# Eight sample sequences computed as a 17th chunk of the prompt's mixer stages

## The reference, cut to what matters

```python
# gated delta rule, for each chunk c of a sequence
m_low = jnp.where(strict, einsum('nbhik,nbhjk->nbhij', kb, k) * decay, 0.0)
sol = triangular_solve(m_low + eye(c), concatenate([v * beta, kb * exp(G)], -1))
v_new = uc - wc @ S                        # S: the state
o = (qc * exp(Gc)) @ S + ac @ v_new        # ac = mask(q k^T) * decay
S = S * exp(g_last) + (kc * exp(g_last - Gc))^T @ v_new
# mLSTM
num = w_inter * (qc @ cs) + s @ vc         # s = (q k^T) * exp(dc - mt)
den = w_inter * (qc @ ns) + sum(s)
cs, ns = a_end * cs + (kc * wk)^T @ vc, a_end * ns + (kc * wk)^T @ 1
```

## Time and profile before

| what | value |
|---|---|
| median of 3 executions | 2635.62 us (2635.26 to 2638.98) |
| the profiled execution, its own time | 2634.22 us |
| its span in the trace | 2632.6 us |
| mean granted TensorE clock | 0.847 of full speed |
| TensorE busy, weight loads busy | 2036.5 us (77%), 1684.9 us (64%) |
| VectorE, ScalarE, GpSimd busy | 1031.5, 488.8, 530.9 us |
| DMA | 117.75 MB, mean 45 GB/s |

### The profile page before, as it was taken

One profiled execution on the slowest core, in us unless ns is written; L12 is line 12 of the kernel. 1 busy time (PEld: TensorE's weight loads), 2 busy tenths in 40 slices (PEclk: granted clock), 3 DMA queues, 4 the chain that ended last, 5 costly groups with the idle time before them and its releaser, 6 DMA issues.

```text
span 2632.6 us, 28198 instructions
## 1 busy us (share of the span) xinstructions
PE 2036.5 (77%) x9888; PEld 1684.9 (64%) x9888; DVE 1031.5 (39%) x1987; ACT 488.8 (19%) x1073; POOL 530.9 (20%) x507
## 2 busy tenths in 40 slices
PE   5877786786534339599869885587899999999996
PEld 3544454454334338588846554464899999999995
DVE  4656665566458957323221401115311111111135
ACT  2211011111312123111120112102320310311311
POOL 0011110111134326110000000000433333433431
PEclk9988888888767669566679996678999999999998
DMA  3000000000042222111151000021111111111111
GB/s 109 32 20 28 18 28 18 18 22 20 10 89 59 39 33 56 62 37 54 36 209 53 32 16 0 26 75 43 34 47 44 44 48 40 48 40 48 48 40 66
DMA packets 65912, 117.75 MB, mean 45 GB/s; under 512 B 18055, under 2 KB 46743, under 8 KB 65143
## 3 DMA queue, kind: packets, MB, share of 16 engines
q1 hardware_dynamic: 62374, 105.21, 13.0%
q0 software_dynamic: 3472, 11.73, 1.4%
HBM read 102.94 MB, written 13.98 MB: 44 GB/s over the span
## 4 chain that ended last, share of the span: by engine, by line
PE 42%; DVE 4%; ACT 2%; DMA 1%; issue 1%; ACTq 0%; DVEq 0%
PE ps L2179 9%; PE ps L2180 9%; PE ps L2181 9%; PE ps L2086 8%; DVE regH L2365 1%; PE ps L2125 1%; PE ps L2112 1%; DVE rows L2363 1%; PE ps L2161 1%; PE ps L2052 1%; PE ps L2119 1%; PE ps L2059 1%; ACT feat L2272 1%; DMA feat<-ck_in 0%; DMA feat<-cv_in 0%
## 5 line engine op out<-in xcount | busy, mean ns | idle before, releaser
L2179 PE MATMUL ps<-feat_r,rows_r 128*128 128x352 f32 x1536 | 501.7, 327 | 31.7 <-DVE regH_r L2370 20.2
L291 PE MATMUL ps<-regH,regW 128*128 128x352 f32 x1296 | 419.5, 483 | 7.3 <-DVE regH L510 7.3
L2181 PE MATMUL ps<-feat_r,regW_r 128*128 128x352 f32 x1152 | 373.9, 325 | 0.0
L291 PEld LDWEIGHTS ps<-regH,regW 128*128 128x128 f32 x1296 | 263.4, 204 | 162.7 <-issue 32.6
L2179 PEld LDWEIGHTS ps<-feat_r,rows_r 128*128 128x128 f32 x1536 | 292.6, 190 | 34.2 <-issue 29.8
L2347 DVE TENSOR_TENSOR regA<-ps,regA 128x352 f32<-128x352 f32 (+1 forms) x144 | 75.5, 524 | 473.7 <-PE ps L2181 304.5
L2180 PE MATMUL ps<-feat_r,rows_r 128*128 128x352 f32 x768 | 249.6, 325 | 0.0
L2180 PE MATMUL ps<-regH_r,rows_r 128*128 128x352 f32 x768 | 248.4, 323 | 0.0
L2181 PEld LDWEIGHTS ps<-feat_r,regW_r 128*128 128x128 f32 x1152 | 220.2, 191 | 0.0
L2036 POOL TENSOR_TENSOR rows_r<-regW,cst 128x1024 fp32r<-128x1024 f32 x48 | 94.5, 1969 | 430.6 <-PE ps L2181 333.9
L2431 DVE TENSOR_TENSOR feat_r<-feat,feat_r x96 | 51.8, 539 | 317.5 <-ACT feat_r L2252 317.5
(11 more groups left out here) (444 smaller groups left out, 3157.7 us busy)
## 6 DMA issues: line engine op xcount, KB each, us to landing
regW<-w_ff_in SPq DMA_DIRECT2D x48, 512.0 KB, 3.5
regW<-w_in_in SPq DMA_DIRECT2D x27, 512.0 KB, 3.4
ext<-w_ff_in SPq DMA_DIRECT2D x16, 512.0 KB, 3.4
regA<-xT_in SPq DMA_DIRECT2D x3, 1408.0 KB, 10.6
regA<-xT_in SPq DMA_DIRECT2D x1, 4224.0 KB, 22.1
yT_out<-regH SPq DMA_DIRECT2D x3, 1408.0 KB, 5.5
feat<-ck_in POOLq DMA_DIRECT2D x8, 512.0 KB, 3.9
feat<-cv_in POOLq DMA_DIRECT2D x8, 512.0 KB, 3.9
```

The lines of the kernel that those rows point to most:

```text
L291: ins = pe.matmul(ps[b][:, 0:BW], ring[slot][:, k * P:(k + 1) * P], hv[:, k, blk(b)], start=(k == 0), stop=(k == KT - 1))
L2179: pe.matmul(ps[b][:, 0:BW], hi, rhs_hi(k, b), start=(k == 0), stop=False)
L2181: ins = pe.matmul(ps[b][:, 0:BW], lo, rhs_hi(k, b), start=False, stop=(k == KT - 1))
```

## The change

The third block goes. The 32 sample tokens become one more chunk of the second block:
- their part of the gates' rows is made in the first block and row_scratch gets T columns; SyncE loads four more spreads of rows (behind ten memsets of POOL) before the ml rows;
- key and query products for the 32 tokens are masked so that only tokens of one sequence meet (pcauss); their MT is a 17th chunk: 34 stores, V of 102 rows, elimination 102 rows high, nine stores of the inverse, and a 17th Yd;
- rows for the samples (s_in, nine DMAs) are loaded beside the elimination, two of them (s_nb) behind the stores of the inverse; the prompt's mLSTM state is stored ahead of the inverse; at chunk 4 all states of the samples are loaded by two DMAs (3.17 MB) in a new layout, the mLSTM's n as a 65th column of each head;
- behind the last chunk a tail treats all eight sequences together: products of 8 columns with the states, the mLSTM's numerator, u from the inverse, masked copies of keys and values (s_kwm, s_vnm, mask pseq), products for the new states, which POOL has scaled and VectorE adds to; the new states go out in one DMA for each mixer. The last unit's norm stands in the middle of this tail;
- the fourth block's norm of the sample tokens is done in the tail; the third block's constants go.

```diff
-        rowsD = nc.dram_tensor("row_scratch", [6, H, SEQ], F32, kind="Internal").ap()
-        mtD, yD = (nc.dram_tensor(n, [2, NC, NP, CW, CW], F32, kind="Internal").ap() for n in ("mt_scratch", "inv_scratch"))
+        rowsD = nc.dram_tensor("row_scratch", [6, H, T], F32, kind="Internal").ap()
+        mtD, yD = (nc.dram_tensor(n, [2 * (NC + 1) * NP, CW, CW], F32, kind="Internal").ap() for n in ("mt_scratch", "inv_scratch"))
...
+        NS = 2 * (NC + 1) * NP
+        V = A(64 * 64)[0:NS, :]
+        vtmp = A(1024)[0:NS, :]
...
+        s_kwm = regA[0:TS, 3072:3072 + DB * NP * P].rearrange("p (s m) -> p s m", s=DB)
...
+        s_qwm = regH[:, 0:NP * DB * (TS + DS)].rearrange("p (n t) -> p n t", n=NP)
+        s_vnm = regH[:, 864:864 + NP * DB * HD].rearrange("p (n s d) -> p n s d", n=NP, s=DB)
...
+        s_S = regW[:, :].rearrange("p (s n m) -> p s n m", s=DB, n=NP)
...
+                q.wait_ge(sem("zero"), 10)
+                for h in range(2):
+                    spread(s_gB, 0, smp, h, "gs_in")
+                    spread(s_nB[:, :, 0:TS], 1, smp, h, "nbs_in")
...
+                q.wait_ge(sem("mt"), UN + 1)
+                for h in range(2):
+                    a = (2 * NC + h) * NP
+                    q.dma_start(mtD[a:a + NP].rearrange("n j i -> j n i"), s_nB[half(h)]).then_inc(sem("mt_out"), 16)
+                q.wait_ge(sem("mt_out"), 34 * 16)
+                q.wait_ge(sem("dk"), UN + 1)
+                q.wait_ge(sem("aT"), UN + 1)
+                q.wait_ge(sem("db"), UN + 1)
+                q.dma_start(V, mtD.rearrange("c j i -> c (j i)")).then_inc(sem("v_in"), 16)
...
+                for h in range(2):
+                    spread(s_e, 2, smp, h, "s_in")
+                    spread(s_gb, 3, smp, h, "s_in")
+                    spread(s_wi, 5, smp, h, "s_in")
+                q.dma_start(s_r1, rowsD[4][:, smp].unsqueeze(0).to_broadcast([TS, H, TS])).then_inc(sem("s_in"), 16)
+                q.wait_ge(sem("Cd"), UN)
+                q.dma_start(o["ml_p"], caug).then_inc(sem("st_out"), 16)
                 q.wait_ge(sem("inv"), 1)
                 for g in range(4):
...
+                q.dma_start(yD[96:NS].rearrange("c j i -> c (j i)"), V[96:NS, :]).then_inc(sem("y_out3"), 16)
                 q.wait_ge(sem("zero2"), 1)
-                for c in range(NC):
-                    if c % 4 == 0:
-                        q.wait_ge(sem(f"y_out{c // 4}"), 32)
...
+                    if c == 4:
+                        q.wait_ge(sem("st_out"), 16)
+                        q.dma_start(s_S, t["dn_s0"].rearrange("p s (n m) -> p s n m", n=NP)).then_inc(sem("s_state_in"), 16)
+                        q.dma_start(s_C, t["ml_c0"].rearrange("p s (n w) -> p s n w", n=NP)).then_inc(sem("s_state_in"), 16)
...
+                q.wait_ge(sem("s_Sd"), 6)
+                q.dma_start(o["dn_s"], s_S).then_inc(sem("st_out"), 16)
+                q.wait_ge(sem("s_Cd"), DB)
+                q.dma_start(o["ml_c"], s_C).then_inc(sem("st_out"), 16)
+                q.wait_ge(sem("st_out"), 64)
...
+                pool.wait_ge(sem("s_in"), 9 * 16)
...
+                signal(pool.tensor_tensor(s_r1, s_r1, pcaus_seq[0:TS].unsqueeze(1).to_broadcast([TS, H, TS]), ALU.add), "s_r1")
...
+                pool.wait_ge(sem("s_state_in"), 32)
+                pool.wait_ge(sem("s_st"), 1)
+                signal(pool.tensor_tensor(s_S, s_S, by_s(s_e)[:, :, :, DS - 1].rearrange("p n s -> p s n").unsqueeze(3)
+                                          .to_broadcast([P, DB, NP, P]), ALU.mult), "s_Sz")
+                pool.wait_ge(sem("s_num"), 1)
+                signal(pool.tensor_tensor(s_C, s_C, by_s(s_wi)[:, :, :, DS - 1].rearrange("p n s -> p s n").unsqueeze(3)
+                                          .to_broadcast([P, DB, NP, 2 * VW]), ALU.mult), "s_Cz")
...
+                pe.wait_ge(sem("kbd"), 2 * UN + 2)
+                pe.wait_ge(sem("mt"), UN - 1)
+                for p in range(NP):
+                    out = ps[0][:, 0:384].rearrange("p (k n t) -> p k n t", k=2, n=NP)[:, :, p, 0:TS]
+                    ins = pe.matmul(out, s_kb[:, p, :], qkv[:, p:p + 4:3, smp], start=True, stop=True)
...
+                pe.wait_ge(sem("s_state_in"), 32)
+                pe.wait_ge(sem("s_kq"), 2)
+                pe.wait_ge(sem("kdec"), NC)
+                for p in range(NP):
+                    for b in range(DB):
+                        ins = pe.matmul(ps[0][:, (p * DB + b) * 8:(p * DB + b + 1) * 8], s_S[:, b, p, :], s_kq[:, p, b, :],
+                                        start=True, stop=True)
...
+                pe.wait_ge(sem("s_qw"), 1)
+                pe.wait_ge(sem("rst"), UN)
+                pe.wait_ge(sem("s_va"), 2)
+                pe.wait_ge(sem("s_sT"), 1)
+                for p in range(NP):
+                    for b in range(DB):
+                        pe.matmul(ps[6][0:TS, p * 2 * VW:(p + 1) * 2 * VW], s_qwm[:, p, b * TS:(b + 1) * TS], s_C[:, b, p, :],
+                                  start=(b == 0), stop=False)
...
+                        ins = pe.matmul(ps[6][0:TS, n * VW:(n + 1) * VW], s_sT[:, n, :], s_vaug[:, n, :], start=False, stop=(h == 1))
+                ins.then_inc(sem("s_num"), 1)
...
+                triple(ps[3], Yd[NC % 3], s_r, "s_u")
...
+                    for p in range(NP):
+                        ins = pe.matmul(ps[spare[b % 3]][:, p * 2 * VW:(p + 1) * 2 * VW], s_kwm[:, b, p * P:(p + 1) * P],
+                                        s_vaug[:, 2 * p:2 * p + 2, :], start=True, stop=True)
+                    ins.then_inc(sem("s_dC"), 1)
...
+                pe.wait_ge(sem("s_vm"), 2)
+                for p, bank in enumerate((4, 5, 2)):
+                    ins = pe.matmul(ps[bank][:, :], kdec[0][:, p, :], s_vnm[:, p, :, :], start=True, stop=True)
+                ins.then_inc(sem("s_dS"), 1)
...
+                    step(dve.tensor_tensor(tmp, v3[:, 0:k, k:k + 1].to_broadcast([NS, k, w]),
+                                           v3[:, k:k + 1, k + 1:64].to_broadcast([NS, k, w]), ALU.mult))
...
+                dve.wait_ge(sem("s_st"), 1)
+                dve.wait_ge(sem("s_tv"), 1)
+                dve.wait_ge(sem("s_ez"), 1)
...
+                    dve.tensor_tensor(by_s(s_rbd[half(h), :, 64 * h:64 * h + TS]), by_s(s_tv[half(h)]), inter[half(h), :, :, 0:DS], ALU.add)\
...
+                dve.wait_ge(sem("s_r1"), 1)
+                dve.tensor_tensor(s_r1, s_r1, mlc[0:TS, UN, 0:6].unsqueeze(2).to_broadcast([TS, H, TS]), ALU.add).then_inc(sem("s_td"), 1)
...
+                dve.tensor_tensor(s_sT, ps[7][0:TS, 0:H * TS].rearrange("p (n t) -> p n t", n=H), s_r1, ALU.mult).then_inc(sem("s_sT"), 1)
+                out_norm(UN - 1, 0)
+                out_norm(UN - 1, 1)
...
+                dve.tensor_tensor(s_kwm, s_kw.rearrange("p n m -> p (n m)").unsqueeze(1).to_broadcast([TS, DB, NP * P]),
+                                  pseq[0:TS].unsqueeze(2).to_broadcast([TS, DB, NP * P]), ALU.mult).then_inc(sem("s_kwm"), 1)
...
+                    dve.tensor_tensor(s_vnm[half(h)], s_vn[half(h), :, half(h)].unsqueeze(2).to_broadcast([64, NP, DB, HD]),
+                                      pseq[half(h)].unsqueeze(1).unsqueeze(3).to_broadcast([64, NP, DB, HD]), ALU.mult)\
+                       .then_inc(sem("s_vm"), 1)
...
+                dve.wait_ge(sem("s_Sz"), 1)
+                dve.wait_ge(sem("s_dS"), 1)
+                for p, bank in enumerate((4, 5, 2)):
+                    for h in range(2):
+                        a = s_S[half(h), :, p, half(h)]
+                        dve.tensor_tensor(a, a, ps[bank][half(h), :].rearrange("p (s d) -> p s d", s=DB), ALU.add).then_inc(sem("s_Sd"), 1)
...
+                dve.wait_ge(sem("s_Cz"), 1)
+                spare = (7, 6, 0)
+                for b in range(DB):
+                    dve.wait_ge(sem("s_dC"), b + 1)
+                    for h in range(2):
+                        w = slice(h * VW, (h + 1) * VW)
+                        add = ps[spare[b % 3]][half(h), 0:H * VW].rearrange("p (n w) -> p n w", n=NP)[:, :, w]
+                        ins = dve.tensor_tensor(s_C[half(h), b, :, w], s_C[half(h), b, :, w], add, ALU.add)
+                    ins.then_inc(sem("s_Cd"), 1)
...
-        A, B = Carve(regA), Carve(regH)
...
-                go(dve, {"S": lambda ch: None, "W": lambda ch: None, "fD": fD, "fM": fM, "L": L, "rM": rM, "rD": rD}, step)
-        clear_semaphores()
...
-                pe.wait_ge(sem("mix_sq"), 2)
-                pe.matmul(ps[6][:, 0:6 * 32], heads, mixsq, start=True, stop=True).then_inc(sem("mix_ps"), 1)
...
-                act.activation(mixsq[:, 0:3, :], qkv[:, 0:3, SEQ:T], ACT.Square).then_inc(sem("mix_sq"), 1)
-                act.activation(mixsq[:, 3:6, :], zml[:, 0:3, SEQ:T], ACT.Square).then_inc(sem("mix_sq"), 1)
-                act.activation(mixden, zml[:, 3:6, SEQ:T], ACT.Square, scale=EPS ** 0.5).then_inc(sem("mix_sq"), 1)
...
```

(2 more changed lines are left out.)

804 lines of the change are left out of this document (265 added, 539 removed).

## The result

The changed kernel takes 2452.43 us (median of 4 executions, 2450.79 to 2453.92) against 2635.44 us: the ratio is 0.9305, 95% interval 0.9289 to 0.9321, so 183 us less. In a later comparison with five executions the ratio was 0.9283 (0.9260 to 0.9305). The forecast was 2453.5.

The account below looks back on a forecast made before the run. The block for eight sequences (245 us) was taken as bound by its chain of small products. Removing 254.6 us, adding 15.4 of prompt-stage delays and a 65 us tail saves 182.1: 2453.5 us, eight in ten 2434 to 2480.

Parts of the forecast that it names:

- load of V: Mixer start, before the elimination: loading 102 rows instead of 96 takes 14 us instead of 9.9, adding 4.1.
- the inverse's way back: Elimination to first Yd product: a ninth store, SyncE's wait for all nine and two s_nb loads add 5.5 us (3 to 9).
- sweep (state loads): Sweep over the prompt's chunks: 3.17 MB loaded at chunk 4 delays decay rows, adding 2 us (0 to 9).
- to the next block: After ml_c's store: clearing and engines meeting took 4.6 us; 49 more names add 1.8, between nothing and 3.5.
- Start of the mixer: Up to the elimination: memset wait and row loads 2.5 us, two more MT stores 1.4, V 4.1; sum 8.0 (3 to 17).
- six engines: Rival, 32%: six of sixteen engines carry V's rows, the load takes 26.4 us, elimination 12.4 later than forecast: 2466 us.
- The tail: From TensorE's last prompt product to the next block's first DMA: 65 us; under 55 or over 75 would be wrong.
- step 3: Tail, numerator: 60 halves of products, 16 slow and 44 fast, 8.0 us (bounds 6 and 12).
- The first term: Tail's start: eight-column products with the states, 48 halves, half at clock 1 and half at 0.5, 8.4 us (6.0 to 10.8).
- Clock: Rival, 1%: the granted clock falls in the feed-forward stage after the change; at 0.80 the kernel takes 2673 us.
- GpSimd holding nothing: Rival, 14%: GpSimd's long scalings don't hold VectorE; tail steps 2 and 4 lose some 5.8 and 5.7 us: 2442.
- States: Rival, 11%: decay rows and Yd in the sweep wait for the whole 3.17 MB of state loads, +9 us: 2462.5.

Follow-up runs that it names:

- the second profile: The changed kernel, unedited, profiled in a second execution: 380.4 us from the mixer's first DMA to the last block's first, against 383.7.
- the experiment with s_nb: Changed kernel with the two s_nb row loads and their wait moved behind the third pair of Yd loads: 2447.39 us.
- all three edits: Changed kernel, singly: s_td ahead of VectorE's wait, 2447.1 us; GpSimd's second scaling after s_vnm, 2449.56; both scalings cut in eight, 2446.27.
- seven edits: Changed kernel with V split, one inverse store, later s_nb, early s_td and exponential, second scaling in eight, shared clearing, ml_c in halves: 2418.57 us.
- the kernel cut in pieces: Changed kernel with both of GpSimd's scalings of all states cut into eight instructions each, one for each sequence: 2446.27 us.

## Why the prediction was right, and where it wasn't

The forecast of 2453.5 came within 1.1 us of the 2452.4 measured, but that closeness is luck: the errors of its terms, without their signs, add up to some 20 us and cancel, and the start of the mixer scatters by several us from one execution to the next. Predicted and measured from the two profiles, in us:

| term | predicted | measured |
|---|---|---|
| gate rows | -0.1 | -0.2 |
| wait for memsets, four row loads | 2.5 | 0.8 |
| two more MT stores and their landing | 1.4 | 0.9 |
| load of V | 4.1 | 7.8 |
| elimination, 102 rows high | 0 | -0.9 |
| the inverse's way back | 5.5 | 3.0 |
| sweep (state loads) | 2.0 | 2.4, none of it the loads |
| products with states | 8.4 | 7.8 |
| to s_sT | 8.5 | 6.6 |
| numerator | 8.0 | 9.1 |
| u, s_vnm | 10.7 | 9.0 |
| state products, additions, norms | 10.4 | 10.9 |
| eight ml states | 6.5 | 8.4 |
| store of ml_c | 6.1 | 5.2 |
| to the next block | 6.4 | 7.8 |

*What bounded the block.* Right: a chain of small products, which eight sequences at once walk only once.

*Start of the mixer.* The wait for ten memsets and the four loads cost 0.8 instead of 2.5. The issue of the ml rows took longer (8.61 us for two, has 5.64), but MT's first store had 1.6 us to spare.

*Load of V.* This is the step that failed most. I took 14 us between 10.5 and 15.9 and gave six engines 32% with 26.4 us. The load takes 17.7, and it does run on six engines. The rival's mechanism was right and its price wrong. The 17.7 us lie outside the 11 to 16 that I gave as the sign of being right, and just under the 18 of being wrong. I scaled the 9.9 us by 16/6, as if all sixteen engines had worked for this load alone in that time. The earlier trace rows had the right number beside it: 224 GB/s on engines that were 92% busy are 15.2 GB/s for each, so six carry 1.67 MB in 18.3 us (near, not exact: where the load was alone, 103 GB/s on 5.4 engines were 19 for each). The elimination took 0.9 us less (0.5 in the second profile); I take it that, starting later, it had less to share its time with, but no run shows that. The time for 12-row stores was read a little high, too: 1.57 MB from 954.1 to 969.4 are 103 GB/s, not 105.

*The inverse's way back.* Mechanism right (the experiment with s_nb), 5.5 against 3.0: ScalarE's wait for the ninth store ended at 981.5 and would have held the product to 983.5 in any case, and Yd's load took less than the 4.6 us of a full queue.

*State loads.* Wrong. They cost nothing at chunk 4. The 2.4 us found in their place lie where the clock rises late, and vary between executions of one kernel. At chunk 13 the loads do cost 6.5 us, the clock's fall in the wait included.

*The tail.* 64.9 for 65.0, and each wait where the prediction put it: s_td ends 0.2 us behind GpSimd's first scaling, and s_vnm 3.4 us behind the second (1104.57 to 1107.97), the time that its two instructions need by themselves. Off were the sizes. GpSimd's scalings take 5.4 us, not 7.2: the 1.80 us of L981 for 768 elements is not a quarter of what 3072 take. The last five ml states take 1.30 us each, 0.72 of VectorE's additions and 0.57 of its wait for TensorE, where the sum had 0.8 a round (and even its own two rates, twice 1.4 and six times 0.75, give 7.3 and not 6.5): with three banks the products and the additions still did not overlap fully. In step 3 sixteen slow halves and 44 fast ones are 8.3 by the rates named, not 8.0; 9.1 were measured. The first term came near for the reason given: the granted clock fell from 1.0 to 0.50 at about 1077.8, 2.5 us into the eight-column products, with TensorE busy throughout.

*To the next block.* Half of the upper bound was too little. And the count was off: the row of before is that of the sample block's 65 names, and the new block has 124, so 59 more, not 49; they cost 3.2 us, 0.055 each.

*The first block.* The changed profile is 3.3 us late at 580 us already, in stages that the change does not touch. Over all profiles the mixer's first DMA goes between 746.5 and 756.6 us (those with the faster clearing gain 2 of that), and in the kernel before at 753.5, so these 3 us are not told from scatter.

*The rivals.* Clock: 0.99 in the feed-forward stage, as before. GpSimd holding nothing: refuted by all three edits. States: possible, but not at chunk 4. Six engines: it happened, at a third of its price (3.7 us over the forecast's term, not 12.4).

## What to carry to other kernels

- When rows are added to a DMA, look at what the new row count does to the number of engines: 102 rows for 96 cost 7.8 us, and 96 and 6 in two DMAs give 5.3 to 5.7 of them back. Price it by the rate of an engine (GB/s over busy share), not by the time of the old transfer.
- An instruction of GpSimd over thousands of elements on the critical stretch holds VectorE's next instruction with both inputs in SBUF, however small. Moving it behind one victim only picks another; cutting it into pieces, or moving the victim ahead, frees the victim, and the next wait then decides what is gained (4.2 us off the addition gave 1.6 at the numerator).
- A stage that is a serial chain for each sequence is shortened by its number of rounds, but what surrounds the chain grows: names to clear, one large store at the end, a wait in a queue that others stand in. Here seven edits to such costs and to the waits on GpSimd gave 29.0 us back together, and two of the costs were in the kernel before as well.

## What the runs showed of the hardware

- A DMA of 102 rows of 16 KB used 0.34 of the sixteen engines where it ran alone and took 17.7 us; with 96 and 6 rows in two DMAs 0.97 were busy in the 6 us shown, and it took 12.0.
- GpSimd holds VectorE's instructions with both inputs in SBUF: 0.34 us became 4.50. It pays, too: its work cut in eight took 7.19 us beside a short addition and 10.27 beside s_vnm (5.37 and 5.42 uncut).
- After 17 us of idling TensorE's granted clock stayed at 0.50 (1.2 GHz) for about 3 us of uninterrupted work in one execution of a kernel and for about 10 in another; in the kernel cut in pieces it was 12. A stage that begins there scatters by 2 to 3 us.
- Clearing a semaphore cost SyncE about 0.055 us; five engines side by side cut 4.3 us from a block end with 124 names.
- 3.17 MB of loads cost the sweep nothing at one chunk and 6.5 us at another, where the load of the inverse issued right behind them took 13 us to arrive.
